# Eight decay levels of a recurrent block: second token half stored reversed, one matmul per head and level, ScalarE takes two levels

## The chip, the cores and the metric

The kernel runs on one core of a Trainium2 chip. The metric is device microseconds of one launch. Three runs of the kernel before gave 1195.58 to 1196.34 us, median 1196.15. The engines named below are PE (TensorE matmul) with PEld (its weight loads), DVE (VectorE), ACT (ScalarE), POOL (GpSimd) and SP, whose queue carries the weight stream from device memory.

## The reference, cut to what matters

Two transformer-like blocks run over 256 tokens of width 1024. The change touches one layer of the second block, the gated linear recurrence:

```python
q, fz, inp, og = jnp.split(h @ w_in, ...)       # 8 heads of 128 features
q = silu(q);  f = lb + (1 - lb) * sigmoid(fz);  k = 1 - f
# S_t = diag(f_t) S_{t-1} + k_t i_t^T ;  o_t = S_t^T q_t, per head
o = rms_norm(o, out_norm) * sigmoid(og)
return o @ w_out
```

Unrolled, a head's output at token t is the sum over s <= t of i_s times the score sum_n q_t[n] k_s[n] exp(cum_t[n] - cum_s[n]), where cum is the running sum of log f. The scores are a 256 x 256 lower triangle for each of 8 heads. The decay differs in each feature n, so it has to be multiplied into the operands ahead of a matmul, and it must be kept from overflowing.

## The kernel before, in words

**Weights.** All weight matrices come as one stream of parts of 128 x 1024 fp32 (512 KB), through a ring of four slots. SP loads a part into `raw`; ACT copies it to `w_hi` in a reduced fp32 form (`hi`, L276); DVE subtracts to get the remainder `w_lo` (`lo`, L679; `step` calls it). PE multiplies with both (three matmuls a block of 128 x 128, L1388 to L1390; for the value tiles, where tokens are the stationary side, L1489 to L1491). DVE makes a part's remainder three parts ahead of the tile with which it is called, and PE's tile waits for it (`lo_ready`). Each engine works through its own list in order; only semaphores tie them together.

**Stages around the change.** The phases are `hf` (forget gate), `hq` (queries), `hi` (values) and `hg` (output gate), 8 parts each, then `ho` (output projection). While PE multiplies `hf` and `hq`, DVE scales their results out of PSUM by the norm factor (`normed`, L715), ACT applies sigmoid or silu, DVE makes the keys (`gate_key`) and the running sums `CUM` (the scans, L1022).

**Levels.** The triangle inside each 128-token half is cut into levels 0 to 7. Level 0 is the diagonal, level 1 the pairs; level l splits the tokens into blocks of 2^l, and scores the later half of a block (queries) against its earlier half (keys), both decayed to the block's middle, so that all exponents stay at or below 0. A last step, `across_mm`, scores the second 128 tokens against the first 128.

For each level from 2 on there are five pieces of work. DVE writes the exponents (`level_args`: L1034 for the queries, L1036 for the keys). ACT takes the exp of the whole 128 x 2048 buffer `EB[l % 2]` (L543). DVE multiplies the queries in (`level_queries`, L1042). PE scores (`level_mm`, L1652): for each head and each token half one matmul, the 128 tokens of `EB` as the stationary tile, the 64 later tokens as the moving columns, 16 matmuls a level into two PSUM banks. DVE copies what belongs to the level from PSUM into the score matrix `PD` (`take`, L1056), a copy predicated by a 0/1 mask, 2 instructions a level.

The order is written out by hand. DVE's round for level l is: `level_args(l)`, `take(l-2)`, a `step`, `level_queries(l)`, from l = 7 on two evictions of `hg` tiles, a `step`. PE's round is two tiles of `hi` or `hg`, then `level_mm(l)`. `level_args(l)` waits until PE is done with level l-2, whose buffer it overwrites. After level 7 PE does `hg_tile(6)`, `across_mm` (L1663) and `hg_tile(7)`; ACT copies the across scores to `PX` (L565); then PE does the head outputs (L1700 to L1702).

PE's first level matmul waits for `column_rstd` (DVE's copy L695, behind the last scan), for the queries and for the keys.

Of the kernel before, what the change touches and what calls it, by code (L numbers as in the profile page):

```python
# [15 lines left out]
I32 = mybir.dt.int32  # L16
# [4 lines left out]
P = 128  # L21
# [47 lines left out]
LEVELS = 8  # L69
# [4 lines left out]
def build(nc, stream, par_d, x_d, wf_d, table_d, onehot_d, ident_d, mask_d, lmask_d, out_d):  # L74
    scr = nc.dram_tensor("bias_rows", [H_MOBA, P, EXT], F32, kind="Internal")
    row = nc.dram_tensor("bias_row", [H_MOBA, EXT], F32, kind="Internal")
    with ExitStack() as ctx:
# [56 lines left out]
        LM = flat(F[:, 48:52, :]).bitcast(I32).rearrange("p (l t) -> p l t", l=LEVELS)  # L134
        EB = [F[:, 0:8, :], F[:, 60:68, :]]
        PD = F[:, 68:76, :].rearrange("p u (z t) -> p (u z) t", z=2)
# [3 lines left out]
        CK, LK = KK, OG  # L140

# [125 lines left out]
        def _(act):  # L267
# [254 lines left out]
            for t in range(C):  # L522
                act.wait_ge(evacuated, TILE["hf"] + t + 1)
                A(FG[:, t, :], FG[:, t, :], ACT.Sigmoid).then_inc(f_raw, 1)
                multiplied(PART["hf"] + t)
                hi(0, 0, PART["hf"] + t + HI_AHEAD)
            for t in range(C):
# [4 lines left out]
                if t == 5:  # L532
                    kodd, eodd = (flat(x).rearrange("p (n b) -> p n b", b=2)[:, :, 1:2] for x in (KK, EB[1]))
                    A(eodd, kodd, ACT.Copy).then_inc(pair_keys, 1)
                act.wait_ge(evacuated, TILE["hq"] + t + 1)
                A(QS[:, t, :], QS[:, t, :], ACT.Silu).then_inc(q_ready, 1)
# [4 lines left out]
            def level_decay(l):  # L541
                act.wait_ge(arg_ready, 2 * (l - 1))
                A(EB[l % 2], EB[l % 2], ACT.Exp).then_inc(dec_ready, 1)  # L543

# [124 lines left out]
        def _(dve):  # L669
# [317 lines left out]
            def gate_key(t):  # L987
                dve.wait_ge(f_raw, t + 1)
                v.tensor_scalar(FG[:, t, :], FG[:, t, :], der[:, D_1LB + t:D_1LB + t + 1],
                                der[:, D_LB + t:D_LB + t + 1], ALU.mult, ALU.add).then_inc(f_ready, 1)  # L990
                dve.wait_ge(f_ready, t + 1)
                v.tensor_scalar(KK[:, t, :], FG[:, t, :], -1.0, 1.0, ALU.mult, ALU.add).then_inc(k_ready, 1)

            def halves(ap, l):

                w = flat(ap).rearrange("p (n b) -> p n b", b=2 ** l)
                return w[:, :, 0:2 ** (l - 1)], w[:, :, 2 ** (l - 1):]
# [3 lines left out]
            for t in range(C):  # L1001
                multiplied(PART["hf"] + t)
                normed(FG[:, t, :], TILE["hf"] + t)
# [3 lines left out]
            for t in range(C):  # L1007
                multiplied(PART["hq"] + t)
                normed(QS[:, t, :], TILE["hq"] + t)
# [3 lines left out]
                if t == 1:  # L1013
                    dve.wait_ge(f_ready, C)
                    dve.wait_ge(k_ready, C)
                    v.tensor_tensor(halves(EB[1], 1)[0], halves(KK, 1)[0], halves(FG, 1)[1],
                                    ALU.mult).then_inc(pair_keys, 1)
# [3 lines left out]
                for c in {2: [0, 1], 3: [2], 4: [3], 5: [4, 5], 6: [6], 7: [7]}.get(t, []):  # L1021
                    v.tensor_tensor_scan(CUM[:, c, :], ONES_ROW, CUM[:, c, :], 0.0, ALU.mult,  # L1022
# [856 lines left out]
```

## Time and profile before

| | us |
|---|---|
| median of three runs | 1196.15 |
| the profiled execution, its own time | 1196.31 |
| its span in the trace | 1194.5 |
| PE busy | 1170.8 (98%) |
| DVE busy | 910.9 (76%) |
| ACT busy | 710.5 (59%) |
| POOL busy | 379.3 (32%) |

PE's granted clock is in the top tenth in all 40 slices of the span. The chain of work that ended last is PE in 90% of its length. Durations of matmuls overlap each other: the time that one costs is the distance from its start to the next one's start. The level stage runs from about 598.5 to 671.8 us after the span's start.

### The profile page before, as it was taken

The numbers are of one execution on the slowest core, as the hardware profiler recorded it, in microseconds if no ns is written. First come the engines' busy times: TensorE is split into PE (matmuls) and PEld (weight loads), VectorE is DVE, ScalarE is ACT, GpSimd is POOL, SyncE is SP. The second block draws the span as 40 slices with busy tenths as digits, with TensorE's granted clock in tenths as the row PEclk, the third lists the DMA queues.
The fourth block names the chain that finished last, engine by engine and source line by source line (L and its number), as shares of the span: only waits on it lengthen the run. The fifth ranks groups of instructions, "written<-read, shape, count | busy, mean of one in ns | idle before, by whom it ended". The sixth has DMA issues, their size and how long they took to land.

```text
span 1194.5 us, 23920 instructions
## 1 busy us (share of the span) xinstructions
PE 1170.8 (98%) x8502; PEld 1099.6 (92%) x8502; DVE 910.9 (76%) x1346; ACT 710.5 (59%) x1129; POOL 379.3 (32%) x397
## 2 busy tenths in 40 slices
PE   8999999999999999998999999999999999999996
PEld 8999989999899999888999988888899999888886
DVE  7866897867699998548898698777666768877754
ACT  6598655554467777445754566666555556666552
POOL 3444000700445555222000135545320006555431
PEclk9999999999999999999999999999999999999999
DMA  6556433376546555562534256556765435655661
GB/s 214 180 191 215 139 124 108 125 269 188 193 119 184 188 178 184 205 193 85 182 107 138 72 161 209 186 184 200 257 196 191 142 111 181 203 179 189 207 201 69
DMA packets 56627, 204.47 MB, mean 171 GB/s; under 512 B 6688, under 2 KB 6840, under 8 KB 56432
## 3 DMA queue, kind: packets, MB, share of 16 engines
q1 hardware_dynamic: 54288, 197.35, 51.1%
q0 software_dynamic: 1696, 5.13, 1.2%
q8 instruction: 47, 0.77, 0.3%
q10 hardware_dynamic: 576, 1.05, 0.2%
q14 instruction: 20, 0.16, 0.0%
HBM read 202.43 MB, written 2.63 MB: 172 GB/s over the span
## 4 chain that ended last, share of the span: by engine, by line
PE 90%; DVE 7%; ACT 1%; DMA 1%; issue 0%; POOL 0%; DVEq 0%; SPq 0%; POOLq 0%; ACTq 0%
PE bank L1382 20%; PE bank L1388 15%; PE bank L1389 14%; PE bank L1390 14%; PE bank L1383 11%; PE bank L1652 2%; PE bank L1385 2%; PE bank L1489 2%; PE bank L1490 2%; PE bank L1491 2%; DVE w_lo L679 2%; DVE h_two L709 1%; PE bank L1576 1%; DVE work L834 1%; DVE work L733 1%; PE bank L1566 1%
## 5 line engine op out<-in xcount | busy, mean ns | idle before, releaser
L679 DVE TENSOR_TENSOR w_lo<-raw,w_hi 128x1024 fp32r<-128x1024 f32 x374 | 477.7, 1284 | 130.2 <-ACT w_hi L276 125.2
L276 ACT ACTIVATE w_hi<-raw 128x1024 fp32r<-128x1024 f32 x374 | 392.0, 1052 | 136.4 <-PE bank L1390 66.0
L1388 PE MATMUL bank<-h_two,w_hi 128*128 128x256 f32 x1184 | 342.4, 289 | 11.4 <-DVE h_two L709 7.5
L1389 PE MATMUL bank<-h_two,w_hi 128*128 128x256 f32 x1184 | 335.6, 283 | 0.0
L1390 PE MATMUL bank<-h_two,w_lo 128*128 128x256 f32 x1184 | 335.5, 283 | 0.0
L1388 PEld LDWEIGHTS bank<-h_two,w_hi 128*128 128x128 f32 x1184 | 227.5, 192 | 17.9 <-issue 9.0
L1389 PEld LDWEIGHTS bank<-h_two,w_hi 128*128 128x128 f32 x1184 | 227.8, 192 | 0.3
L1390 PEld LDWEIGHTS bank<-h_two,w_lo 128*128 128x128 f32 x1184 | 227.6, 192 | 0.0
L1382 PE MATMUL bank<-h_two,w_hi 128*128 128x512 f32 x616 | 221.5, 398 | 1.0 <-DVE h_two L709 1.0
L1383 PE MATMUL bank<-h_two,w_lo 128*128 128x256 f32 x704 | 183.6, 281 | 0.0
L1382 PE MATMUL bank<-u_two,w_hi 128*128 128x512 f32 x455 | 161.0, 397 | 0.0
L1383 PEld LDWEIGHTS bank<-h_two,w_lo 128*128 128x128 f32 x704 | 132.9, 189 | 7.9
L1382 PEld LDWEIGHTS bank<-h_two,w_hi 128*128 128x128 f32 x616 | 115.9, 188 | 25.6 <-DVE h_two L709 1.3
L1383 PE MATMUL bank<-u_two,w_lo 128*128 128x256 f32 x476 | 130.4, 281 | 0.1
L1388 PE MATMUL bank<-u_two,w_hi 128*128 128x256 f32 x392 | 112.1, 286 | 0.5 <-DVE u_two L1103 0.4
L1390 PE MATMUL bank<-u_two,w_lo 128*128 128x256 f32 x392 | 110.9, 283 | 0.0
L1389 PE MATMUL bank<-u_two,w_hi 128*128 128x256 f32 x392 | 110.9, 283 | 0.0
L1319 POOL TENSOR_TENSOR work<-work 128x256 f32<-128x256 f32 x68 | 52.7, 776 | 173.3 <-DVE work L1162 114.6
L1382 PEld LDWEIGHTS bank<-u_two,w_hi 128*128 128x128 f32 x455 | 85.4, 188 | 19.8
L1324 POOL TENSOR_TENSOR u_two<-work,u_two 128x256 f32 x68 | 98.5, 1449 | 12.5 <-POOL u_two L1322 12.5
L285 ACT ACTIVATE work<-bank 128x256 f32<-128x256 f32 x109 | 41.4, 380 | 95.0 <-PE bank L1385 95.0
L1383 PEld LDWEIGHTS bank<-u_two,w_lo 128*128 128x128 f32 x476 | 89.8, 189 | 2.4 <-POOL u_two L1324 0.5
(244 smaller groups left out, 1851.8 us busy)
## 6 DMA issues: line engine op xcount, KB each, us to landing
raw<-in_stream SPq DMA_DIRECT2D x374, 512.0 KB, 3.6
bias_rows<-bias_row POOLq DMA_DIRECT2D x1, 1536.0 KB, 15.2
work<-in_x_t SPq DMA_DIRECT2D x2, 512.0 KB, 6.2
work<-in_x_t POOLq DMA_DIRECT2D x1, 1024.0 KB, 5.7
work<-bias_rows POOLq DMA_DIRECT2D x1, 1024.0 KB, 11.1
out<-work ACTq DMA_DIRECT2D x4, 256.0 KB, 2.4
work<-in_lmask POOLq DMA_DIRECT2D x1, 512.0 KB, 7.3
work<-bias_rows POOLq DMA_DIRECT2D x1, 512.0 KB, 6.5
```

Source lines behind the costliest of these rows:

```text
L276: A(w_hi[:, slot, :], raw[:, slot, :], ACT.Copy).then_inc(hi_ready, 1)
L285: A(LOW[:, t % BANKS, :], bank[t % BANKS][:, S:2 * S], ACT.Copy).then_inc(low_out, 1)
L679: v.tensor_tensor(w_lo[:, slot, :], raw[:, slot, :], w_hi[:, slot, :].bitcast(F32), ALU.subtract).then_inc(lo_ready, 1)
L1319: g.tensor_tensor(PB[:, pair, :], GB[:, pair, :], YB[:, 2 * pair + 1, :], ALU.mult).then_inc(pair_free, 1)
L1324: g.tensor_tensor(dst_l, PB[:, pair:pair + 1, :], dst_h.bitcast(F32), ALU.subtract).then_inc(ul_ready, 1)
L1382: mm(pair, w_hi[:, slot, s], both, start=start, stop=False)
L1383: last = mm(own, w_lo[:, slot, s], r_two[:, 0, :], start=False, stop=False)
L1385: last = mm(pair, w_hi[:, slot, s], both, start=False, stop=True)
L1388: mm(out, w_hi[:, slot, s], r_two[:, 0, :], start=start, stop=False)
L1389: mm(out, w_hi[:, slot, s], r_two[:, 1, :], start=False, stop=False)
L1390: return mm(out, w_lo[:, slot, s], r_two[:, 0, :], start=False, stop=stop)
L1489: mm(out, h_hi[:, b, ts], w_hi[:, s0:s0 + 2, f], start=(b == 0), stop=False)
```

## The change

The second 128 tokens of the forget gate, keys, queries and running sums are stored in reversed order, each half of 8 heads x 128 in one piece (index z is the half, c the head). In the reversed half, the later tokens of every block lie where the earlier ones lie in the first half. So the earlier tokens of half 0 and of half 1 interleave to a full set of 128 positions. For levels 2 to 7 the exponents of the keys of both halves are written into one packed stationary tile per head, and those of the queries of both halves into one packed moving block of 128 columns: `level_mm` has 8 matmuls a level instead of 16. Each gives the scores of both halves, and cross terms that are not taken. Levels 0 and 1 (`pair_mm`) stay at 16 matmuls.

What this asks for elsewhere: `normed` of `hf` and `hq` becomes two instructions of 128 columns, the second written backwards (`normed_halves`); each scan becomes two of 128, the second run backwards. POOL makes a reversed copy of the second half of the normed input `h_two` (8 copies of 128 x 2 x 128 into a free part of `u_two`) and of the norm factor row; the value tiles of the second token half use it. `across_mm` and the second head output read a moving operand backwards. The running sums of the second half start at zero, so level 8's exponents need one DVE instruction instead of two, and two ACT exps of 1024 columns instead of one of 2048. The takes of levels 6 and 7 move from DVE to ACT (`take_wide`): plain copies of 32-row and 64-row pieces without a mask, 8 for level 6 and 4 for level 7. The masks of the other six levels are stored packed (64 columns for each half).

```diff
+        def early(u, l):
+            h = 2 ** (l - 1)
+            return units(u, 0, [[C * P + h, 2], [2 * h, C * P // (2 * h)], [1, h]])
+        def later(u, l):
+            h = 2 ** (l - 1)
+            return units(u, h, [[C * P - h, 2], [2 * h, C * P // (2 * h)], [1, h]])
+        def packed_keys(u, l):
+            h = 2 ** (l - 1)
+            return units(u, 0, [[h, 2], [2 * h, C * P // (2 * h)], [1, h]])
+        def packed_queries(u, l):
+            h = 2 ** (l - 1)
+            return units(u, C * P, [[C * P // 2, 2], [h, C * P // (2 * h)], [1, h]])
...
+                    A(EB_T[0][:, 0, :, :], EB_T[0][:, 0, :, :], ACT.Exp)
+                    A(EB_T[0][:, 1, :, :], CUM_T[:, 1, :, :], ACT.Exp).then_inc(dec_ready, 1)
...
+            def take_wide(l):
+                b = 2 ** l
+                h = b // 2
+                for g in range(2):
+                    act.wait_ge(lev_sel, 2 * l + g)
+                    act.wait_ge(lev_mm, 2 * l + g + 1)
...
+                            last = A(PD_T[rows, z, 4 * g:4 * g + 4, cols], src[rows, z, :, n * h:(n + 1) * h], ACT.Copy)
+                    last.then_inc(lev_sel, 1)
...
+            take_wide(6)
             gate_tile(4)
             gate_tile(5)
+            take_wide(7)
...
+            def normed_halves(dst, c, t):
+                v.tensor_tensor(dst[:, 0, c, :], out_of(t)[:, 0:P], RSTD[:, 0:P], ALU.mult)
+                v.tensor_tensor(dst[:, 1, c, ::-1], out_of(t)[:, P:S], RSTD[:, P:S], ALU.mult).then_inc(evacuated, 1)
...
-                    v.tensor_tensor_scan(CUM[:, c, :], ONES_ROW, CUM[:, c, :], 0.0, ALU.mult,
-                                         ALU.add).then_inc(hcum_ready, 1)
+                    for sums in (CUM_T[:, 0, c, :], CUM_T[:, 1, c, ::-1]):
+                        ins = v.tensor_tensor_scan(sums, ONES_ROW[:, 0:P], sums, 0.0, ALU.mult, ALU.add)
+                    ins.then_inc(hcum_ready, 1)
...
+            def args_later(l):
+                v.tensor_tensor(packed_queries(U_EB[l % 2], l), later(U_CUM, l), middle(U_CUM, l),
+                                ALU.subtract).then_inc(arg_ready, 1)
+            def args_earlier(l):
+                v.tensor_tensor(packed_keys(U_EB[l % 2], l), middle(U_CUM, l), early(U_CK, l),
+                                ALU.subtract).then_inc(arg_ready, 1)
...
-                take(l - 2)
+                if l - 2 < TAKEN:
+                    take(l - 2)
...
-            take(LEVELS - 1)
             step("hg", 6)
...
+            for c in range(C):
+                pool.wait_ge(hl_ready, H_COUNT["n0"] + c + 1)
+                g.tensor_copy(H_REV[:, c, :, :], h_two[:, c, :, P:S][:, :, ::-1]).then_inc(h_turned, 1)
+            pool.wait_ge(rstd_ready, NORMS["n0"] + 1)
+            g.tensor_copy(RSTD_REV, RSTD[:, P:S][:, ::-1]).then_inc(rstd_turned, 1)
...
             def level_mm(l):
...
+                keys = EB_T[l % 2][:, 0, :, :]
+                queries = EB_T[l % 2][:, 1, :, :].rearrange("p c t -> p (c t)").rearrange("p (z c j) -> p z c j", z=2, c=C)
+                pe.wait_ge(x_up, l - 1)
                 for g in range(2):
+                    pe.wait_ge(lev_sel, 2 * (l - 2) + g + 1)
+                    out = bank[4 + 2 * (l % 2) + g][:, :].rearrange("p (z c j) -> p z c j", z=2, c=4)
+                    for c in range(4 * g, 4 * g + 4):
+                        last = mm(out[:, :, c % 4, :], keys[:, c, :], queries[:, :, c, :], start=True, stop=True)
                     last.then_inc(lev_mm, 1)
```

On PE, this is level 2 of the kernel before with the first matmuls of the value tile behind it; the number ahead of each line of code is a row's place in PE's list, and `level_taken` and `level_queries` are the semaphores of the takes and of the queries.

```order
3029 L1491 MATMUL bank3<-w_lo,h_two 128x256
3030 L1652 MATMUL bank4<-work 128x64 [waits level_taken,level_queries]
3031 L1652 MATMUL bank4<-work 128x64 x7
3032 L1652 MATMUL bank5<-work 128x64 [waits level_taken]
3033 L1652 MATMUL bank5<-work 128x64 x7
3034 L1489 MATMUL bank0<-w_hi,h_two 128x256 [waits evacuated,lo_ready]
```

The same place on PE in the changed kernel:

```order
3029 L1562 MATMUL bank3<-w_lo,u_two 128x256
3030 L1728 MATMUL bank4<-work 128x2x64 [waits level_taken,level_queries]
3031 L1728 MATMUL bank4<-work 128x2x64 x3
3032 L1728 MATMUL bank5<-work 128x2x64 [waits level_taken]
3033 L1728 MATMUL bank5<-work 128x2x64 x3
3034 L1560 MATMUL bank0<-w_hi,h_two 128x256 [waits evacuated,lo_ready]
```

Eight matmuls of 128 columns stand where sixteen of 64 stood; the value tile behind them waits for the same remainder (`lo_ready`) as before.

On DVE, these are the last query eviction and scan of the kernel before, the copy that releases PE's first level matmul (`column_mm` is its wait), and the rounds of levels 3 and 7.

```order
524 L715 TENSOR_TENSOR work<-bank3,work 128x256 [waits part_done]
525 L679 TENSOR_TENSOR w_lo<-raw,w_hi 128x1024 [waits hi_ready]
526 L1022 SCALAR_TENSOR_TENSOR work<-work 128x256
527 L695 COPY derived<-bank4 128x2 [waits column_mm]
...
536 L1034 TENSOR_TENSOR work<-work 128x256x4 [waits level_mm]
537 L1036 TENSOR_TENSOR work<-work 128x256x4
538 L1056 COPY_PREDICATED work<-work,bank6 128x512 [waits level_mm,level_taken]
539 L1056 COPY_PREDICATED work<-work,bank7 128x512 [waits level_mm,level_taken]
540 L679 TENSOR_TENSOR w_lo<-raw,w_hi 128x1024 [waits hi_ready]
...
575 L1056 COPY_PREDICATED work<-work,bank4 128x16x32 [waits level_mm,level_taken]
576 L1056 COPY_PREDICATED work<-work,bank5 128x16x32 [waits level_mm,level_taken]
```

The same places on DVE in the changed kernel, with level 8's round whole:

```order
539 L1052 TENSOR_TENSOR work<-bank3,work 128x128 [waits part_done]
540 L1053 TENSOR_TENSOR work<-bank3,work 128x128
541 L734 TENSOR_TENSOR w_lo<-raw,w_hi 128x1024 [waits hi_ready]
542 L1078 SCALAR_TENSOR_TENSOR work<-work 128x128 x2
543 L750 COPY derived<-bank4 128x2 [waits column_mm]
...
552 L1082 TENSOR_TENSOR work<-work 128x1024 [waits level_mm]
553 L1086 TENSOR_TENSOR work<-work 128x2x128x4
554 L1119 COPY_PREDICATED work<-work,bank6 128x2x256 [waits level_mm,level_taken]
555 L1119 COPY_PREDICATED work<-work,bank7 128x2x256 [waits level_mm,level_taken]
556 L734 TENSOR_TENSOR w_lo<-raw,w_hi 128x1024 [waits hi_ready]
...
589 L1093 TENSOR_TENSOR work<-work 128x1024 [waits level_mm]
590 L734 TENSOR_TENSOR w_lo<-raw,w_hi 128x1024 [waits hi_ready]
```

Two more instructions stand ahead of the copy L750 in this piece; the round of level 3 has the same five instructions in other shapes; level 8's round has lost an exponent instruction and both takes.

On ACT, this is where the changed kernel has its twelve new copies (L595), among the weight copies (L310) and ahead of the sigmoid of the output gate (L616) and the copies to `PX` (L620).

```order
460 L578 ACTIVATE work<-work 128x1024
461 L595 ACTIVATE work<-bank4 32x4x32 [waits level_mm,level_taken]
462 L595 ACTIVATE work<-bank4 32x4x32 x3
463 L595 ACTIVATE work<-bank5 32x4x32 [waits level_mm,level_taken]
464 L595 ACTIVATE work<-bank5 32x4x32 x3
465 L310 ACTIVATE w_hi<-raw 128x1024 [waits part_landed2,part_done]
466 L310 ACTIVATE w_hi<-raw 128x1024 [waits part_landed3,part_done]
467 L595 ACTIVATE work<-bank6 64x4x64 [waits level_mm,level_taken]
468 L595 ACTIVATE work<-bank6 64x4x64
469 L595 ACTIVATE work<-bank7 64x4x64 [waits level_mm,level_taken]
470 L595 ACTIVATE work<-bank7 64x4x64
471 L616 ACT_TABLE_LOAD
```

In the kernel before, the two weight copies stand directly between level 8's exp and the table load.

## Rows read from the trace of the kernel before

**Rows 1.** The page's head: span; busy time, share, instructions.

```profile
span 1194.5 us, 23920 instructions
PE 1170.8 (98%) x8502; PEld 1099.6 (92%) x8502; DVE 910.9 (76%) x1346; ACT 710.5 (59%) x1129; POOL 379.3 (32%) x397
```

**Rows 2.** Level stage: length, busy (count) of PE, PEld, DVE, ACT, POOL, PE's clock, DMA.

```profile
598.50:671.84 73.34, 73.34 (x632) 73.34 (x632) 60.45 (x61) 35.65 (x36) 0.00 (x0) 1.00 0.36 118
```

**Rows 3.** Chain of work that ended last: start us, us, what.

```profile
598.62 3.52 PE bank L1652 x32
...
667.47 1.79 PE bank L1663 x16
```

**Rows 4.** PE in order of time: start, us, line, form, count.

```profile
614.23 3.68 PE L1652 MATMUL bank<-work 128*128 128x64 f32 x32
617.72 0.36 PE L1489 MATMUL bank<-w_hi,h_two 128*128 128x256 f32 x1
...
632.88 3.68 PE L1652 MATMUL bank<-work 128*128 128x64 f32 x32
...
667.30 1.95 PE L1663 MATMUL bank<-work 128*128 128x128 f32 x16
```

**Rows 5.** DVE ahead of the level stage, in order of time.

```profile
589.50 1.22 DVE L679 TENSOR_TENSOR w_lo<-raw,w_hi 128x1024 fp32r<-128x1024 f32 x1
590.63 0.69 DVE L1022 TENSOR_TENSOR_SCAN work<-work 128x256 f32<-128x256 f32 x1
591.23 0.40 DVE L715 TENSOR_TENSOR work<-bank,work 128x256 f32<-128x256 f32 x1
591.54 1.22 DVE L679 TENSOR_TENSOR w_lo<-raw,w_hi 128x1024 fp32r<-128x1024 f32 x1
```

**Rows 6.** DVE in the level stage; in brackets idle time before, and its releaser.

```profile
597.96 0.14 DVE L695 COPY derived<-bank 128x2 f32<-128x2 f32 x1
...
602.18 1.32 DVE L1056 COPY_PREDICATED work<-work,bank 128x512 f32<-128x512 int32 x1 [0.39 <-PE bank L1652]
...
611.73 1.22 DVE L1034 TENSOR_TENSOR work<-work 128x1024 f32<-128x1024 f32 x1
...
614.00 2.47 DVE L1056 COPY_PREDICATED work<-work,bank 128x512 f32<-128x512 int32 x2
616.26 1.27 DVE L679 TENSOR_TENSOR w_lo<-raw,w_hi 128x1024 fp32r<-128x1024 f32 x1
...
624.25 1.28 DVE L679 TENSOR_TENSOR w_lo<-raw,w_hi 128x1024 fp32r<-128x1024 f32 x1
...
629.96 1.33 DVE L1056 COPY_PREDICATED work<-work,bank 128x512 f32<-128x512 int32 x2
631.16 1.23 DVE L679 TENSOR_TENSOR w_lo<-raw,w_hi 128x1024 fp32r<-128x1024 f32 x1
...
645.93 1.22 DVE L1034 TENSOR_TENSOR work<-work 128x1024 f32<-128x1024 f32 x1 [2.35 <-PE bank L1652]
```

**Rows 7.** ACT: level 8's exp, and a copy to `PX`.

```profile
657.65 1.92 ACT L543 ACTIVATE work<-work 128x2048 f32<-128x2048 f32 x1 [4.86 <-DVE work L1036]
...
669.29 0.60 ACT L565 ACTIVATE work<-bank 128x512 f32<-128x512 f32 x1 [0.24 <-PE bank L1663]
```

**Rows 8.** POOL's last instruction ahead of the level stage.

```profile
552.15 0.73 POOL L1228 TENSOR_TENSOR work<-work 128x256 f32<-128x256 f32 x1 [1.61 <-ACT work L303]
```

**Rows 9.** DVE: the remainder for `hf`'s fifth tile.

```profile
558.84 1.23 DVE L679 TENSOR_TENSOR w_lo<-raw,w_hi 128x1024 fp32r<-128x1024 f32 x1 [1.10 <-ACT w_hi L276]
```

**Rows 10.** PE: the first matmul of `hf`'s fifth tile.

```profile
560.24 0.34 PE L1388 MATMUL bank<-h_two,w_hi 128*128 128x256 f32 x1
```

**Rows 11.** POOL's copies of 256 columns: count, min/median/max ns, first and last start.

```profile
L1322 POOL CAST u_two<-work x68: 396/398/1388, 343.6 to 1126.0; 128x256 f32 x68
```

**Rows 12.** POOL: an instruction that meets one of DVE's.

```profile
741.97 1.72 POOL L1324 TENSOR_TENSOR u_two<-work,u_two 128x256 f32 x1 [0.18 <-POOL u_two L1322]
```

**Rows 13.** DVE: the instruction that meets it.

```profile
743.02 0.95 DVE L1162 TENSOR_TENSOR work<-work 128x256 f32<-128x256 f32 x1
```

More of the change, by code:

```diff
@@ L532, in _ @@
                 if t == 5:
[L533 to L534 removed]
+                    A(later(U_EB[1], 1), later(U_KK, 1), ACT.Copy).then_inc(pair_keys, 1)
                 act.wait_ge(evacuated, TILE["hq"] + t + 1)
[L536 removed]
+                A(QS_T[:, :, t, :], QS_T[:, :, t, :], ACT.Silu).then_inc(q_ready, 1)
                 multiplied(PART["hq"] + t)
@@ L1015, in _ @@
                     dve.wait_ge(k_ready, C)
-                    v.tensor_tensor(halves(EB[1], 1)[0], halves(KK, 1)[0], halves(FG, 1)[1],
-                                    ALU.mult).then_inc(pair_keys, 1)
+                    v.tensor_tensor(early(U_EB[1], 1), early(U_KK, 1), later(0, 1), ALU.mult).then_inc(pair_keys, 1)
                 if t == 2:
@@ L1047, in take @@
                 h = b // 2
[L1048 removed]
+                n = P // b
                 for g in range(2):
@@ L1072, in _ @@
             dve.wait_ge(ck_ready, 1)
-            level_args(2, later=False)
+            args_earlier(2)
             level_queries(2)
@@ L1442, in columns @@
                 pe.wait_ge(rstd_ready, NORMS[norm] + 1)
+                if norm == "n0":
+                    pe.wait_ge(rstd_turned, 1)
                 for tok in range(2):
-                    last = mm(bank[4][:, S + tok:S + tok + 1], RSTD[0:1, tok * P:(tok + 1) * P], ones[0:1, 0:1],
-                              start=True, stop=True)
+                    row = RSTD_REV[0:1, :] if tok and norm == "n0" else RSTD[0:1, tok * P:(tok + 1) * P]
+                    last = mm(bank[4][:, S + tok:S + tok + 1], row, ones[0:1, 0:1], start=True, stop=True)
                 last.then_inc(col_mm, 1)
@@ L1863 @@
     s, t = np.arange(P)[:, None], np.arange(P)[None, :]
-    lmask = np.stack([s == t, (s >> 1 == t >> 1) & (s <= t)]
-                     + [(s >> l == t >> l) & (s >> (l - 1) != t >> (l - 1)) & (s < t)
-                        for l in range(2, LEVELS)], axis=1).astype(np.int32)
+    later_keys = []
+    for l in range(TAKEN):
+        b = 2 ** max(l, 1)
+        h = b // 2
+        for z in range(2):
+            q = np.array([n * b + i + (h if (l > 0) != (z == 1) else 0) for n in range(P // b) for i in range(h)])[None, :]
+            same = s // b == q // b
+            later_keys.append(s == q if l == 0 else same if l == 1 else same & ((s // h) % 2 == z))
+    lmask = np.stack(later_keys, axis=1).astype(np.int32)
     arrays = {"stream": stream, "par": par, "x_t": x_t, "wf": wf,
```

123 lines of the change are left out of this document (68 added, 55 removed).

## The prediction

> **What bounds the kernel now.** I read the page's head first: PE is busy for 1170.8 of 1194.5 us [rows 1], so only what PE does, or waits for, can move the time much. The windows view of the level stage then shows 73.34 of 73.34 us busy on PE at the full clock of 2.4 GHz, with 60.45 us on DVE and 35.65 on ACT [rows 2]. PE has no gap there, but DVE is the close second. Third, the chain of waits: in this stretch it is PE throughout, and one level is a piece of 3.52 us [rows 3]. Last, the order in time of PE, DVE and ACT, to see how early each of DVE's results comes before PE needs it.
>
> The chain gives the price of a level matmul. A level is 32 recorded matmuls (two for each of the 16 in the code) of 64 columns in 3.52 us, 0.110 us each; the across step is 16 recorded matmuls of 128 columns in 1.79 us, 0.112 each [rows 3, 4]. Twice the columns cost the same: at 64 columns the pace is not set by the columns.
>
> **The term on PE.** Levels 2 to 7 go from 32 recorded matmuls of 64 columns to 16 of 128. By the across step's row that is 3.52 - 1.79 = 1.73 us a level, 6 x 1.73 = 10.4 us. Levels 0 and 1 and the across step keep count and size. That a moving operand in two pieces costs nothing is shown by L1489, whose two weight slots lie apart and which runs at the usual pace; for an output in two pieces the trace has no row (rival D).
>
> **What delays the first level.** Two things stand ahead of it.
>
> The first is the start of `hf`'s fifth tile. DVE's remainder for it begins at 558.84 after a wait for ACT, ends at 560.07, and PE starts the tile at 560.24 with a stretched first matmul [rows 9, 10]: no slack. Ahead of that remainder `normed` is now two instructions. A DVE instruction of 1024 columns takes 1.13 us from start to start, one of 256 takes 0.31 [rows 5]: 1.07 ns a column and 0.04 to 0.07 us for the instruction. So a split adds about 0.07. POOL's nine reversed copies start at 552.9, behind its last sum [rows 8]. A copy of 256 columns takes 0.40 undisturbed and 1.39 at worst [rows 11]; 8 x 0.46 = 3.7 us would end them at 557 to 559, if POOL isn't held up by DVE's work there. POOL and DVE do hold each other up: at 741.97 a POOL subtraction took 1.72 us, and the DVE instruction of 256 columns that began under it took 0.95 [rows 12, 13], where an eviction of 256 columns takes 0.40 [rows 5]. The remainder of 558.84 may meet the last copy, for up to 0.4 us. I take 0.3 for both, with bounds of 0.1 and 1.5 (copies at 1.39 each run past 564, and the tight remainder waits for one of them).
>
> By the Trainium skill (SBUF — State Buffer, the section on its two separate sides) a GpSimd instruction and a DVE one with two SBUF inputs exclude each other for a whole instruction. The pair of rows above agrees.
>
> The second is DVE's backlog. From 587.4 to 598.1 DVE runs without a pause, and the copy that PE's level 0 waits for is its last item, at 597.96 [rows 6]. PE starts level 0 at 598.46, which is 0.36 after the copy's end. In that run 5 evictions and 6 scans are split: 11 x 0.067 = 0.73 us. The copy ends at 598.83, PE starts about 0.1 later: 0.49 us of stall. If an element read or written backwards cost double, the second halves would add 5 x 0.13 + 6 x 0.27 = 2.3 us more; no row shows one, so I take no extra and keep 2.3 for the range.
>
> **What the rounds of DVE allow.** PE gets faster than DVE can supply. PE's round for a level was 5.83 us of tiles and 3.49 of level (614.23 to 617.72), now 5.83 and 1.79, together 7.62. DVE's round for levels 3 and 4 is two exponents, two takes, two remainders, one product: 5 x 1.134 + 2.26 = 7.93 us; the row pair 616.26 and 624.25 shows 7.99 between two rounds [rows 6]. For levels 5 to 7 the two takes need 1.20 (629.96 to 631.16) and the round 6.87, plus 0.66 for two evictions in level 7; level 8's loses one exponent and the takes, about 4.1 with its evictions. So DVE is the slower in two rounds. Each arrival, from the kernel before's times:
>
> - DVE's chain is late by 0.49 from the first take on, since its second half waits for PE's level 0 (602.18 in before).
> - The remainder for the tile behind level 2 ended at 617.53 and PE needed it at 617.72 [rows 4, 6]: a slack of 0.2 us. Now it ends at 618.02 and PE, done with level 2 at 614.23 + 0.49 + 1.79 = 616.51, waits till 618.07. Stall 1.56.
> - PE ends level 3 at 618.07 + 5.84 + 1.79 = 625.70. The remainder for the next tile ends at 625.53 + 0.49 = 626.02. Stall 0.37.
> - Level 4 starts at 626.07 + 5.83 = 631.90, against 632.88 in before: 0.98 gained so far.
> - From here DVE's 6.87 is inside PE's 7.62, its rounds start at 628.2, 635.1 and 641.9, and the products are ready 5 us ahead of levels 5 to 7. The tightest arrival is the eviction of `hg`'s first tile at 648.3, which PE needs at 648.9. In before DVE waited up to 2.35 us a round here [rows 6]; that slack is what is used up. Levels 4 to 7 each give 1.70: 6.8 us.
>
> Sum for the stage: 0.98 + 6.8 = 7.8 us, less the 0.3 of `hf`: 7.5.
>
> **ACT's copies.** They are on ACT between level 8's exp and the copies to `PX`, which the heads wait for. Two exps of 1024 columns instead of one of 2048 add one fixed cost. ACT takes 1.92 us for 2048 columns and 0.60 for 512 [rows 7], so 0.86 ns a column and 0.16 fixed: 0.27 for 128 columns, 0.38 for 256. Eight and four of them make 3.7 us at most. From the exp's end at 652.8: level 6's copies till 654.9, two weight copies till 657.0, level 7's till 658.5, table load and sigmoid (they were 1.28 and 1.49) till 661.3, one weight copy till 662.3, `PX` till 663.5. PE reaches the heads at 664.1: hidden, with 0.6 us to spare (2.0 in before). If each copy took the 0.60 of a 512-column one, PE would wait 1 to 3 us for `PX`. The remainder for `ho`'s first part moves behind level 6's copies, but is needed only after the heads begin.
>
> **Nothing for** the packed masks (128 KB less of one early load), the mask copies that DVE loses (counted in its rounds), the reversed reads of the across step and the heads (16 + 16 recorded matmuls; at double pace 32 x 0.11 = 3.5 us, kept for the range). Everything behind the stage is unchanged and moves forward with it.
>
> **The sum.** 1196.31 - 7.5 = 1188.8 against the profiled execution's own time (span 1194.5 to 1187.0). The median of the runs lies 0.16 below that execution: 1188.6.
>
> **Rivals.**
>
> *A. The masked copies get fast, and DVE never holds PE up.* A take of runs of one or two elements costs 1.13 us, of runs of four or more 0.60 (614.00 against 629.96) [rows 6]. The masks are now packed and read in one run. If the mask's stride was what cost, rounds 3 and 4 are 6.87 too and the stalls of 1.56 and 0.37 go: 10.4 - 0.3 - 0.5 = 9.6, so 1186.6. Against it: the destination keeps its short runs.
>
> *B. Backwards is dear, or POOL's copies are.* The bounds above: 2.3 on DVE, 1.2 more in `hf`, 3.5 on PE. One or two of them leave 3 to 6 us of gain; I take 1192.0.
>
> *C, the other side: DVE's new patterns run at half pace.* L1034, L1036 and L1042 now walk two halves, blocks and runs, and the doubling of the takes shows that DVE has patterns at half pace. Three instructions a round would each cost 1.07 more: rounds of 11.1, 11.1, 10.1, 10.1 and 10.7, 53 us against 46.6 for PE's five rounds before. With the late start and what level 7 and the last round give back, some 7 us slower: 1203. It decides from the point where DVE's round passes the 9.32 of PE's old one, which is when these three cost 72% more in the rounds of 6.87. Against it: in before they took 1.22 to 1.24 at every level, whatever the run length.
>
> *D. The merged matmul costs as much as the two.* Each writes two runs of 64 columns 1 KB apart in PSUM. If the pace doubled to 0.22 us, levels cost 3.52 again, and 0.8 us of delays stay: 1197.0. Against it, 128 moving columns took 0.112 in the across step, with a single output run. The Trainium skill (SBUF — State Buffer, the SBUF cachelines note under the DMA port swizzle) says that any non-contiguous PSUM pattern slows matmuls significantly. No row here shows such an output; by that rule the time would be D's.
>
> **How the numbers follow.** Forecast 0.58, A 0.14, B 0.15, C 0.06, D 0.07. The forecast's own range is 1187.4 to 1190.0. The range of 8 in 10 goes from A's 1186.2 into B, to 1191.8: 0.58, 0.14 and half of B are inside. No change means within 0.2%, or 2.4 us, which is about what a measurement can tell. Faster is forecast, A and nearly all of B, 0.86; within 0.2% is most of D and the rest of B, 0.07; slower is C and a part of D, 0.07.
>
> **What would show it.** In the changed trace: 16 recorded level matmuls at 0.112 us for levels 2 to 7; PE waiting for DVE's copy ahead of level 0 (0.5 us) and for remainders behind levels 2 and 3 (1.6 and 0.4), and for nothing in levels 4 to 7; the rounds of DVE at 7.9 twice and then PE's at 7.6; PE's wait for `PX` at zero. The forecast is wrong if PE's level piece isn't about 1.8 us, if the takes of levels 1 and 2 are at 0.60, if scans or evictions run backwards take over 0.4 and 0.25 us, or if the gain is in another stage.

## The result, and the profile after

| | median of the runs | profiled execution: span | PE busy | DVE busy |
|---|---|---|---|---|
| before | 1195.99 us (1195.58 to 1196.34, 4 runs) | 1194.5 | 1170.8 | 910.9 |
| after | 1188.41 us (1187.75 to 1188.77, 4 runs) | 1186.8 | 1161.3 | 908.3 |

The changed kernel takes 0.9935 of the time of the kernel before (95% interval 0.9923 to 0.9947): 7.6 us less, where 7.5 were forecast. A second series, with five runs of the changed kernel beside nine of before, gave 1187.67 us and 0.9929 (0.9915 to 0.9942).

The head of the page after, against [rows 1]:

```profile
span 1186.8 us, 23771 instructions
PE 1161.3 (98%) x8406; PEld 1089.4 (92%) x8406; DVE 908.3 (77%) x1365; ACT 713.8 (60%) x1142; POOL 383.9 (32%) x406
```

PE has exactly 96 matmuls fewer, six levels times 16, and is 9.5 us less busy. 7.7 us of that are in the span; the rest became idle time. The table by stretches of the level stage in the kernel after, from the first matmul of level 0 to the first of the heads (length; then busy time and count of PE, PEld, DVE, ACT, POOL; PE's clock, DMA share, GB/s), beside [rows 2]:

```profile
599.45:664.42 64.97, 63.37 (x538) 62.99 (x537) 56.78 (x56) 39.04 (x49) 0.00 (x0) 1.00 0.42 132
```

The same stretch was 73.50 us before (598.46 to 671.96), with PE busy throughout; now it is 64.97, and PE idles for 1.60 of them. PE in order of time in the kernel after (start, duration, line and form, count; in brackets the idle time ahead and what ended it), against [rows 4]:

```profile
596.48 0.38 PE L1560 MATMUL bank<-w_hi,h_two 128*128 128x256 f32 x1 [0.36 <-DVE w_lo L734]
...
599.45 3.75 PE L1715 MATMUL bank<-work 128*128 128x64 f32 x32
...
615.28 1.95 PE L1728 MATMUL bank<-work 128*128 128x128 f32 x16
...
618.63 0.39 PE L1560 MATMUL bank<-w_hi,h_two 128*128 128x256 f32 x1 [1.40 <-DVE w_lo L734]
...
624.49 1.95 PE L1728 MATMUL bank<-work 128*128 128x128 f32 x16
...
626.63 0.39 PE L1560 MATMUL bank<-w_hi,h_two 128*128 128x256 f32 x1 [0.19 <-DVE w_lo L734]
...
632.48 1.95 PE L1728 MATMUL bank<-work 128*128 128x128 f32 x16
634.19 0.36 PE L1456 MATMUL bank<-h_two,w_hi 128*128 128x256 f32 x1
...
664.42 0.45 PE L1776 MATMUL bank<-work 128*128 128x128 f32 x2
```

The first bracket lies at the first value tile, ahead of level 0; the other two are all the waits of PE from level 0 to the heads. A bracket counts from the modelled end of the last matmul, which is later than the moment at which a next one could have started: behind level 4, where nothing holds PE, the next matmul starts 634.19 - 632.48 = 1.71 us behind the level's first, not 1.95. Counted as the prediction counts, with 1.79 for the level, the two waits behind levels 2 and 3 are 618.63 - 615.28 - 1.79 = 1.56 and 626.63 - 624.49 - 1.79 = 0.35; with 1.71 they are 1.64 and 0.43. The chain that ended last, in the kernel after (start, length, what), where [rows 3] had 3.52 us a level:

```profile
615.15 2.38 DVE work L1119 x2
617.53 1.05 DVE w_lo L734
...
632.65 1.79 PE bank L1728 x16
640.19 1.79 PE bank L1728 x16
...
659.93 1.79 PE bank L1738 x16
```

At level 2 the chain is no longer on PE but on DVE's two masked copies (L1119) and the remainder (L734) behind them. In fact it has no piece on PE from 603.23, at level 0, to 626.63, behind level 3: it runs over DVE and for a few us over ACT, so in this third of the stage DVE's work sets the time, although PE waits for only 2 us of it. From level 4 on it is PE's alone: 7.54 us from level to level.

### The profile page after: what moved, and what is told of

Same layout as the page of the kernel before. It is cut to its first block, busy times and chain, and to the rows that moved or that the text cites. A ratio compares the mean times of both kernels' runs of the same rounds, so it can differ in the third digit from the quotient of the medians.

```text
span 1186.8 us, 23771 instructions
## 1 busy us (share of the span) xinstructions
PE 1161.3 (98%) x8406; PEld 1089.4 (92%) x8406; DVE 908.3 (77%) x1365; ACT 713.8 (60%) x1142; POOL 383.9 (32%) x406
## 4 chain that ended last, share of the span: by engine, by line
PE 87%; DVE 9%; ACT 2%; issue 1%; DMA 1%; POOL 0%; DVEq 0%; SPq 0%; ACTq 0%; POOLq 0%
PE bank L1450 20%; PE bank L1456 14%; PE bank L1458 14%; PE bank L1457 14%; PE bank L1451 11%; DVE w_lo L734 2%; PE bank L1453 2%; PE bank L1560 2%; PE bank L1561 2%; PE bank L1562 2%; DVE h_two L764 1%; PE bank L1647 1%; DVE work L889 1%; DVE work L788 1%; PE bank L1637 1%
## 5 line engine op out<-in xcount | busy, mean ns | idle before, releaser
L734 DVE TENSOR_TENSOR w_lo<-raw,w_hi 128x1024 fp32r<-128x1024 f32 x374 | 477.4, 1284 | 133.2 <-ACT w_hi L310 128.8
L310 ACT ACTIVATE w_hi<-raw 128x1024 fp32r<-128x1024 f32 x374 | 391.6, 1052 | 133.6 <-PE bank L1458 62.5
```

Of the source, the lines that this page charges most:

```text
L310: A(w_hi[:, slot, :], raw[:, slot, :], ACT.Copy).then_inc(hi_ready, 1)
L734: v.tensor_tensor(w_lo[:, slot, :], raw[:, slot, :], w_hi[:, slot, :].bitcast(F32), ALU.subtract).then_inc(lo_ready, 1)
```

## The experiments

Seven kernels beside a second measurement of the changed one. The kernel before was measured again beside each group, with medians of 1196.23 to 1196.43. The two series of the changed kernel, 1188.41 and 1187.67, are 0.7 us apart, so smaller differences between medians say nothing. To compare stages, times are also taken from DVE's reciprocal of the norm ahead of the gates (555.20 in before, 555.72 in after) to the first matmul of the heads: 116.76 us before, 108.70 after, 108.69 in the second series. This leaves out drifts ahead of the stage, which the change does not touch: the reciprocal of the second series is at 554.49.

**The changed kernel again.**

> The changed kernel again, unaltered, as the yardstick of this group. Expected 1188.4 us, 7.6 below the kernel before.

1187.67 us (1187.27 to 1188.07, 5 runs). The waits were 0.35, 1.39 and 0.19 us at the same three places. The pattern is stable.

**PE's term: two matmuls a head and level again.**

```diff
-    last = mm(out[:, :, c % 4, :], keys[:, c, :], queries[:, :, c, :], start=True, stop=True)
+    for z in range(2):
+        last = mm(out[:, z, c % 4, :], keys[:, c, :], queries[:, z, c, :], start=True, stop=True)
```

> The change with one part undone: at levels 2 to 7 each head's merged 128-column matmul is again two of 64 columns with the same stationary tile (16 of each bank pair's worth a level more: 96 matmuls in all become 192); layouts, reversal, takes and order stay the changed kernel's. Theory (the gain is TensorE's, the price of 16 against 32 matmuls a level, 1.79 against 3.52 us): each of the six levels costs 1.73 us more, the waits of 1.39 and 0.19 us behind levels 2 and 3 go, since VectorE gets 1.73 us a level more, while the 0.36 us at the first value tile stays: 10.4 - 1.6 = 8.8 us over the changed kernel, about 1196.5 us, range 1195.7 to 1197.2, which is the kernel before plus the stall. Rival 1 (part of the gain comes from elsewhere, such as cheaper takes and operands read in packed runs): clearly under 1195 us. Rival 2 (a repeated load of the same tile is cheaper): pairs under 0.22 us, chain levels below 3.5 us.

1197.01 us (1196.46 to 1197.31, 10 runs), ratio to before 1.0006 (0.9997 to 1.0015). PE in order of time in this kernel:

```profile
599.45 3.73 PE L1715 MATMUL bank<-work 128*128 128x64 f32 x32
...
615.28 3.68 PE L1729 MATMUL bank<-work 128*128 128x64 f32 x32
...
624.61 3.68 PE L1729 MATMUL bank<-work 128*128 128x64 f32 x32
...
673.02 0.39 PE L1777 MATMUL bank<-work 128*128 128x128 f32 x2
```

Reciprocal to heads: 673.02 - 555.71 = 117.31, which is the 116.76 of before and 0.55 more. Everything else of the change was in place: reversal, packed layout, split evictions and scans, ACT's copies. So the whole gain is PE's, and all the rest together costs 0.5 us, nearly all of it ahead of level 0 (43.74 us behind the reciprocal against 43.26). The waits behind levels 2 and 3 are gone here (624.61 - 615.28 is the 9.33 of before). They exist only because PE got faster. The second matmul with the same stationary tile was no cheaper: 3.52 us a level in the chain. The trace has a weight load for each of the 192 recorded matmuls, so the tile was loaded again every time; whether the load or something else of a matmul sets the pace of 0.11 us, no run separates.

**The waits behind levels 2 and 3: the remainder ahead of the masked copies, in rounds 3 and 4.**

```diff
     level_args(l)
+    if l <= 4: step("hi", n)
     if l - 2 < TAKEN: take(l - 2)
-    step("hi", n)
+    if l > 4: step("hi", n)
```

> In DVE's rounds for levels 3 and 4 the first weight remainder stands ahead of the two takes. Theory (the stall behind levels 2 and 3 is that remainder, queued behind slow takes): both waits of PE (1.40 and 0.19 us idle in the changed kernel's trace, 1.6 and 0.3 counted to the restart) vanish, and level 4 starts about 1.9 us earlier against level 2 than in the changed kernel. But DVE does no less work, so its evictions of the output gate's first tiles stay where they were (648.6 us), and PE, which now asks for them at 647.5, waits about 1.3 us there; ACT's copies to PX, 0.15 us ahead of the heads now, hold the rest. Net gain against the changed kernel 0.1 to 0.5 us. Rival (the two waits are all that DVE costs, nothing behind them is tight): the whole 1.9 us arrive, 1186.5 us.

1188.45 us (1187.92 to 1188.51), ratio 0.9933 (0.9919 to 0.9947). Of this kernel, PE's wait and then the DVE eviction that it was for:

```profile
622.64 1.95 PE L1731 MATMUL bank<-work 128*128 128x128 f32 x16
...
630.18 1.95 PE L1731 MATMUL bank<-work 128*128 128x128 f32 x16
...
649.02 0.36 PE L1459 MATMUL bank<-h_two,w_hi 128*128 128x256 f32 x1 [1.81 <-DVE work L770]
...
664.28 0.46 PE L1779 MATMUL bank<-work 128*128 128x128 f32 x2
```

```profile
648.45 0.75 DVE L770 TENSOR_TENSOR work<-bank,work 128x256 f32<-128x256 f32 x2
```

The two waits vanished and one of 1.81 took their place: the eviction of `hg`'s first tiles is at 648.45, and PE, now about 2 us earlier, needs their banks at 647.2. DVE's work ahead of that eviction is the same, whatever its order. Moving the remainder only moves the wait. From reciprocal to heads it is 664.28 - 555.55 = 108.73, no gain over 108.69. The theory's mechanism held and the rival's 1.9 us did not come; its net gain of 0.1 to 0.5 us did not come either, and the wait was 1.81 where about 1.3 was expected. The last tenth went where the theory said: PE started the across step 0.08 us earlier behind the reciprocal than in the second series, but the heads came 4.78 us behind it instead of 4.66, 0.14 behind the end of ACT's copies to `PX` (664.14).

**ACT's share: VectorE takes all eight levels** (`TAKEN = 8`, no `take_wide`).

> DVE takes all eight levels again, ACT none; the packed matmuls stay. Theory: DVE has 2.3 us of idle time in the round of level 8 and ACT's twelve copies (3.8 us) were hidden by only 0.15 us, so it makes no difference: within 0.4 us of the changed kernel. Rival (moving two takes to ACT is part of the gain, since DVE is the second bound): 1.2 to 2.5 us slower than the changed kernel.

1188.41 us (1187.82 to 1188.58), ratio 0.9934 (0.9921 to 0.9948). The waits behind levels 2 and 3 are again 1.39 and 0.19, and the heads come 0.61 us later than in the second measurement of the changed kernel, like the reciprocal. The median is 0.7 us above the second series, where at most 0.4 was expected, but in the traces the difference lies ahead of the reciprocal: inside the stage both take 108.69. ACT's part of the change is worth nothing here.

**Order and ACT's share together.** DVE takes level 6 too; the remainder stands ahead of the masked copies in all rounds; the evictions come straight behind the exponents in rounds 7 and 8 (not in the cut below); and `columns(2)` and one scan move off the backlog's end.

```diff
-LEVELS, TAKEN = 8, 6
+LEVELS, TAKEN = 8, 7
-            take_wide(6)
+                if t == C - 1: columns(2)
-                for c in {2: [0, 1], 3: [2], 4: [3], 5: [4, 5], 6: [6], 7: [7]}.get(t, []):
+                for c in {2: [0, 1], 3: [2], 4: [3], 5: [4], 6: [5, 6], 7: [7]}.get(t, []):
...
-                if l - 2 < TAKEN: take(l - 2)
                 step("hi", n)
+                if l - 2 < TAKEN: take(l - 2)
                 level_queries(l)
```

> Four moves on DVE and ACT, no new arithmetic: the remainder ahead of the takes in every round; the evictions of the output gate's tiles first in the rounds of levels 7 and 8; DVE takes level 6 (seven masks), ACT level 7 alone; in the query stage one scan moves behind a remainder and the copy that PE's level 0 waits for stands ahead of the last scan. Theory: removes the waits behind levels 2 and 3 (1.9 us), the one ahead of the first value tile (0.36) and the two that would replace them (eviction, PX). By the rows of the changed kernel PE reaches the heads 1.9 us earlier: 1186.5 us, between 1186.0 and 1187.4. Rival: DVE as a whole is at its limit, a new wait eats the gain, within 0.5 us of the changed kernel.

**1185.40 us** (1185.08 to 1185.71, 4 runs), ratio 0.9910 (0.9895 to 0.9925): faster than both kernels, by 2.3 us than the changed one. The table by stretches and PE's order in this kernel:

```profile
598.00:661.03 63.03, 63.03 (x540) 63.03 (x539) 58.30 (x60) 37.42 (x42) 0.00 (x0) 1.00 0.43 136
```

```profile
598.24 3.68 PE L1715 MATMUL bank<-work 128*128 128x64 f32 x32
...
614.01 1.95 PE L1728 MATMUL bank<-work 128*128 128x128 f32 x16
...
621.55 1.95 PE L1728 MATMUL bank<-work 128*128 128x128 f32 x16
...
661.03 0.39 PE L1776 MATMUL bank<-work 128*128 128x128 f32 x2
```

PE never idles in the stage. Reciprocal to heads is 661.03 - 554.92 = 106.11, 2.58 less than the changed kernel's 108.69. Level 0 comes 43.32 us behind the reciprocal instead of 43.73, and each level from 3 on 7.54 behind the last, where the first trace of the changed kernel has 9.21 from level 2 to 3 and 7.99 from 3 to 4: 0.41, 1.67 and 0.45, 2.5 in all. The remainder alone only moved the wait; with the other moves beside it, it is gone. What each move gives by itself no run shows.

**Why the masked copies of levels 1 and 2 are slow: another destination.** Levels 1 and 2 write packed into a free buffer; their scores are missing from the result.

```diff
+    if l in (1, 2):
+        dst = (att_s, att_pt)[g][:, :, :].rearrange("p b e -> p (b e)")[:, 0:512].rearrange(
+            "p (z c n i) -> p z c n i", z=2, c=4, i=h)
```

> The takes of levels 1 and 2 write their 512 columns packed into a free buffer instead of every second or every second pair of columns of the score matrix; these two levels' scores are therefore left out of the result. Mask, source, order and counts are the changed kernel's. Theory (the short runs of the destination, one or two elements, are what makes the masked copies of these levels take 1.23 us each against 0.65 at level 3): they take 0.60 to 0.70 each, VectorE is 1.1 us earlier after each of the two levels, the wait of 1.39 us behind level 2 falls to about 0.3 or less and the 0.19 behind level 3 to nothing: 1186.2 to 1186.7 us against the changed kernel's 1187.7. Rival (the mask, read through a broadcast over four heads with a short inner run, sets the pace, or the kind of copy): the copies stay at 1.2 us and the waits and the time do not move, 1187.4 to 1188.0.

1186.68 us (1186.53 to 1186.96, 4 runs), ratio 0.9919 (0.9904 to 0.9934), 1.0 less than the changed kernel. DVE's masked copies of level 1 in this kernel, and the same in the changed one:

```profile
614.87 0.73 DVE L1122 COPY_PREDICATED att_s<-work,bank 128x512 f32<-128x512 int32 x1
615.49 0.73 DVE L1122 COPY_PREDICATED att_pt<-work,bank 128x512 f32<-128x512 int32 x1
616.10 1.22 DVE L734 TENSOR_TENSOR w_lo<-raw,w_hi 128x1024 fp32r<-128x1024 f32 x1
```

```profile
615.06 2.46 DVE L1119 COPY_PREDICATED work<-work,bank 128x512 f32<-128x512 int32 x2
617.33 1.25 DVE L734 TENSOR_TENSOR w_lo<-raw,w_hi 128x1024 fp32r<-128x1024 f32 x1
```

0.62 us from start to start instead of 1.13, with mask, source and count unchanged. The edit changes the buffer as well as the runs, but level 3 writes the old buffer in runs of four and takes 0.61 (631.04 to 632.26 for two). So the short runs of the destination are the cause. PE's wait behind level 2 fell from 1.39 to 0.33, and the one behind level 3 is gone. Reciprocal to heads: 107.16, or 1.53 less.

**GpSimd's copies beside VectorE, tripled.**

```diff
+    g.tensor_copy(u_two[:, 2 * C + c, :, P:S], h_two[:, c, :, P:S][:, :, ::-1])
+    g.tensor_copy(u_two[:, C + c, :, 0:P], h_two[:, c, :, P:S][:, :, ::-1])
     g.tensor_copy(H_REV[:, c, :, :], h_two[:, c, :, P:S][:, :, ::-1]).then_inc(h_turned, 1)
```

> GpSimd makes each of the eight reversed copies of the hidden state three times, the extra ones into parts of the same buffer that nothing reads: 24 copies instead of 8, about 11.5 us instead of 3.8, from 553.3 to about 565 us, so that they lie beside VectorE's rescales and weight remainders of the first gate tiles. Theory of the prediction (copies that meet VectorE's remainders slow them and each other, and the reversed copy that the second half of a tile waits for comes late): the last copy that TensorE needs (the eighth) is ready about 8 us later, and the tile that first reads it and the remainders beside it lose 0.3 to 2.5 us, so 1188.0 to 1190.2 us beside the changed kernel's 1187.7. Rival (all of it is hidden, since only a share of GpSimd's free time is used): no difference, 1187.4 to 1188.0, and no new idle time ahead of the gate tiles.

1192.59 us (1191.42 to 1194.13, 10 runs), ratio 0.9969 (0.9960 to 0.9979): 4.9 us more than the changed kernel, twice the upper end of what was expected: the mechanism was the one expected, its price was not. The profiled execution is the slowest of the ten (1194.13). Of this kernel POOL, then DVE, then PE, in order of time:

```profile
552.92 1.39 POOL L1406 CAST u_two<-h_two 128x256 fp32r<-128x256 f32 x1
...
559.11 0.41 POOL L1406 CAST u_two<-h_two 128x256 fp32r<-128x256 f32 x1
...
561.88 0.41 POOL L1408 CAST u_two<-h_two 128x256 fp32r<-128x256 f32 x1
562.22 1.36 POOL L1410 COPY work<-work 128x128 f32<-128x128 f32 x1
```

```profile
555.30 1.75 DVE L755 RECIPROCAL work<-work 128x256 f32<-128x256 f32 x1 [1.24 <-ACT work L324]
...
559.01 4.41 DVE L734 TENSOR_TENSOR w_lo<-raw,w_hi 128x1024 fp32r<-128x1024 f32 x1 [1.04 <-ACT w_hi L310]
```

```profile
563.56 0.58 PE L1458 MATMUL bank<-h_two,w_hi 128*128 128x256 f32 x1 [3.05 <-DVE w_lo L734]
563.94 0.42 PE L1459 MATMUL bank<-h_two,w_hi 128*128 128x256 f32 x1
564.15 0.41 PE L1460 MATMUL bank<-h_two,w_lo 128*128 128x256 f32 x1
```

The remainder issued at 559.01 did not run between two of POOL's copies. It ended at 563.42, 1.13 us behind the last of them (562.28): its own undisturbed length. POOL's next copy, of 128 columns, follows at 562.22 like the ones before it, but took 1.36: here DVE had its turn first. PE waited 3.05 us, and afterwards its clock was lower. By stretches:

```profile
563.56:569.06 5.50, 5.50 (x25) 5.50 (x26) 4.78 (x12) 2.74 (x4) 0.02 (x1) 0.50 0.63 188
```

PE had been idle for 3.05 us, and then ran for 5.5 us at 0.50 of its clock, the level of 1.2 GHz: 0.213 us from matmul to matmul instead of 0.120, so 25.8 x 0.093 = 2.4 us. Wait and clock make 5.5, and from reciprocal to heads this execution lost 5.68 against the changed kernel.

**The same, doubled, with the extra copies forwards.**

```diff
+    g.tensor_copy(u_two[:, 2 * C + c, :, P:S], h_two[:, c, :, P:S])
     g.tensor_copy(H_REV[:, c, :, :], h_two[:, c, :, P:S][:, :, ::-1]).then_inc(h_turned, 1)
```

> Ahead of each of the eight reversed copies GpSimd makes one more copy of the same 256 elements, forwards, into a part of the buffer that nothing reads: 16 copies instead of 8. With three copies each, one 1024-column remainder of VectorE that began at 559.01 us took 4.41 us instead of 1.23 and ended 1.13 us after GpSimd's last copy (562.28), TensorE waited 3.05 us and its clock fell. Theory (VectorE's operation with two inputs in SBUF gets no turn while GpSimd's copies follow each other without a pause, and runs its full 1.1 us after the last of them): eight copies more at 0.35 to 0.40 us end at about 558.9 us on the changed kernel's scale, the remainder due at 558.2 runs until about 560.0 (1.8 us instead of 1.23), TensorE waits at most 0.3 us for it, the clock stays full: 1187.5 to 1188.4 us against the changed kernel's 1187.7. Rival (the two share the port in proportion, or each copy costs the time anew): half of the 4.9 us that three copies cost, about 1190 us. Forward and reversed copies take the same 0.40 us each if the direction costs nothing; if reversed ones are dearer, the two lines of the profile differ.

1188.92 us (1188.51 to 1189.29, 4 runs), ratio 0.9938 (0.9921 to 0.9955). By the medians of the two series that is 1.2 us more than the changed kernel, 0.5 above the theory's range and 1.1 below the rival's 1190. POOL, DVE and PE in this kernel:

```profile
558.62 0.40 POOL L1406 CAST u_two<-h_two 128x256 fp32r<-128x256 f32 x1
558.97 0.40 POOL L1407 CAST u_two<-h_two 128x256 fp32r<-128x256 f32 x1
559.31 0.30 POOL L1409 COPY work<-work 128x128 f32<-128x128 f32 x1
```

```profile
558.87 1.82 DVE L734 TENSOR_TENSOR w_lo<-raw,w_hi 128x1024 fp32r<-128x1024 f32 x1 [1.04 <-ACT w_hi L310]
```

```profile
560.82 0.38 PE L1457 MATMUL bank<-h_two,w_hi 128*128 128x256 f32 x1 [0.46 <-DVE w_lo L734]
```

Again the remainder ended (560.69) 1.1 us behind POOL's last copy (559.61), this time the one of 128 columns, which went ahead of it. It took 1.82 us, as the theory had it; PE waited 0.46 where at most 0.3 was expected, and no slow stretch followed (PE's clock is at 1.00 in the 6 us behind it). Reciprocal to heads is 109.30, 0.61 more than the changed kernel. The execution profiled is the fastest of the four, which leaves the other 0.6 of the 1.2 us without a cause on record. Forward (L1406) and reversed (L1407) copies both take 0.40 us.

## Why the prediction was right, point by point

- *PE's term, 6 x 1.73.* Right, and a little low. The chain has 1.79 us a level, as forecast. In the group of all 96 matmuls the output in two runs 1 KB apart made no difference (count; minimum, median and maximum ns; first and last start):

```profile
L1728 PE MATMUL bank<-work x96: 272/275/275, 615.3 to 656.8; 128*128 128x128 f32 x96
```

  1.79 / 16 is 0.112 us each, as in the across step. That refutes rival D. The note of the Trainium skill that stood behind it (SBUF — State Buffer, the cachelines note under the DMA port swizzle) does not hold for this pattern: a PSUM output in two runs of 64 fp32 did not slow these matmuls. Shorter runs, and matmuls whose pace the columns set, were not tried. Undoing only this part gave back 9.3 us by the medians (1197.01 against 1187.67), of which 117.31 - 108.69 = 8.62 lie between reciprocal and heads.
- *`hf`: 0.3 us.* Mis-sized on the safe side. The eight copies ran from 553.34 to 557.16 and the tight remainder began at 559.43, so they did not meet. Measured from the reciprocal this remainder began 0.07 us later than before (3.71 against 3.64), the price of a split, and PE started the fifth tile 0.03 later (5.07 against 5.04). The bound of 1.5 rested on copies of 1.39 each; only the first one took that, behind a remainder that took 1.76 before and after, and it cost nothing.
- *DVE's backlog: 0.49 us ahead of level 0.* The size was right, the place was not. The copy that PE's level 0 waits for ended 43.57 us behind the reciprocal, 0.67 later than before, where 0.73 stood: the prediction counts 5 split evictions in this run of DVE, the trace has 4, and with the 6 scans 10 x 0.067 is 0.67. DVE after, ahead of the level stage, against [rows 5]:

```profile
592.42 1.22 DVE L734 TENSOR_TENSOR w_lo<-raw,w_hi 128x1024 fp32r<-128x1024 f32 x1
593.55 1.37 DVE L1078 TENSOR_TENSOR_SCAN work<-work 128x128 f32<-128x128 f32 x4
594.83 0.27 DVE L1052 TENSOR_TENSOR work<-bank,work 128x128 f32<-128x128 f32 x1
595.01 0.28 DVE L1053 TENSOR_TENSOR work<-bank,work 128x128 f32<-128x128 f32 x1
595.21 1.22 DVE L734 TENSOR_TENSOR w_lo<-raw,w_hi 128x1024 fp32r<-128x1024 f32 x1
```

  PE waited at the first value tile for the remainder of 595.21, queued behind four scans, and not 3 us later at the copy of the columns. Level 0 began 43.73 us behind the reciprocal instead of 43.26: 0.47 for this term and `hf`'s together, where 0.79 stood.
- *Backwards costs nothing, 2.3 us kept in the range.* Right. L1053 writes backwards in 0.28 us, with 0.20 to the next start; L1052 writes forwards in 0.27, with 0.18; POOL's copies take 0.40 either way; the reversed moving operands of the across step keep 1.79 for 16. Rival B had these three as its bounds.
- *The waits of 1.56 and 0.37 us behind levels 2 and 3.* Right to 0.02 us: measured, with the prediction's 1.79 for the level, 1.56 and 0.35, at the places and for the releaser named. They came from subtracting the time of DVE's round, which the change leaves as it was (2.46 for the two takes against 2.47 [rows 6]), from PE's, which it shortens. Rival A needed the takes to get fast by the packed mask. They did not, and its counter-argument, that the destination keeps its short runs, was shown to be the cause by the packed destination.
- *Rival C.* Did not come: the packed two-run operands of DVE kept 1.20 to 1.24 us for 1024 columns at every level.
- *Levels 4 to 7: 1.70 us each, and the tightest arrival at `hg`'s first tile.* The mechanism was right, the size 0.08 too small. A round of PE is 7.54 us, not 7.62, against 9.32 before: 1.78 each. The prediction took 3.49 us of the old level from start to start, but 1.79 of the new one from the chain; from start to start the new one is 1.71. PE did not wait for the eviction in the changed kernel. That it was the next limit was shown when the remainder was moved: once PE came about 2 us earlier, it waited 1.81 us for exactly this eviction. (The 4.1 us for DVE's round of level 8 is a slip: two remainders, an exponent, a product and two evictions make 4 x 1.134 + 0.66 = 5.2. Nothing hung on it.)
- *ACT's copies: hidden, 0.6 us to spare.* Right, with less room. ACT after, in order of time, where [rows 7] had the copies to `PX` far from the end:

```profile
653.55 2.24 ACT L595 ACTIVATE work<-bank 32x128 f32<-32x128 f32 x8
...
657.84 1.57 ACT L595 ACTIVATE work<-bank 64x256 f32<-64x256 f32 x4
...
663.18 1.09 ACT L620 ACTIVATE work<-bank 128x512 f32<-128x512 f32 x2
```

  The copies cost 3.8 us (3.7 was the estimate), but `PX` ended at 664.27, 0.15 us ahead of the heads at 664.42. From the reciprocal, `PX` came 0.25 us later than worked out and the heads 0.2 earlier.
- *The sum, 7.5 us.* From reciprocal to heads it was 116.76 - 108.70 = 8.06, so the stage gave 0.56 more than forecast. Up to the start of level 4 (632.88 before, 632.48 after) it gave 0.92, where 0.98 - 0.3 = 0.68 stood: most of the 0.3 for `hf` was not there. From there to the heads it gave 7.14 instead of 6.8, the 0.08 of each level. Against it the stretch ahead of the reciprocal, which the change does not touch, was 0.52 us later in that execution (in the second series it was earlier), and 0.16 came back behind the heads. The closeness of 1188.6 to 1188.41 is partly luck: errors of half a us each way that cancel.

## What to carry to other kernels

When a change makes the bounding engine faster, write down the round of each engine that feeds it, before and after: the wait is their difference, and here it came out to a few hundredths from rows of the old trace. Take both rounds on the same clock, from start to start. A wait taken away at one place moves to the next tight arrival if the feeder's total work ahead of that stays the same; look for that arrival first, and reorder up to it (here evictions, a scan, the copy of the columns and the takes of level 6 as well as the remainder: 2.3 us for all of them together). An edit that is free because it is hidden can be a few copies away from a cliff: eight GpSimd copies cost nothing that could be measured, 16 cost 0.6 to 1.2 us, 24 cost 4.9.

## What the runs showed of the hardware

- A DVE operation with two inputs in SBUF (the on-chip memory) can be kept out by a whole row of GpSimd copies. Issued at 559.01 with nine more copies of 0.35 us to come, it got no turn between them and ended 1.13 us behind the last one; issued at 558.87 with two to come, 1.1 us behind. It is no rule for every GpSimd instruction that follows without a pause: in the first case a tenth, of 128 columns, came behind the DVE operation, and the row's first copy also let a DVE remainder pass. What decides it, no run shows. In the same copies' time DVE's reciprocal, with one input, took its normal 1.75 us, and evictions from PSUM their 0.28. The Trainium skill (SBUF — State Buffer, its two separate sides) has the pair of ports locked for a whole instruction, by whichever starts first. These traces agree on who is locked out, and show more: the wait can last for many instructions, not for one.
- The first copy of the row took 1.39 us instead of 0.40 in these kernels and in the changed one, behind a DVE remainder under way: the exclusion works in both directions.
- A wait of 3.05 us was followed by 5.5 us of PE at 1.2 GHz. In this stage it cost 2.4 us on top of itself; waits of 1.81, 1.40 and 0.46 us were followed by none.
- A masked copy of 512 fp32 columns takes 1.13 us into a destination whose runs are one or two elements long, and 0.62 into a packed one, with the same mask and source.
- Recorded fp32 matmuls with 64 and with 128 moving columns take 0.110 and 0.112 us from start to start, also when the output lies in two runs of 64 or the moving operand is read backwards.
